# Layer norms of a transformer block: the steps of Pool and ScalarE moved to VectorE, and the low parts of xT taken ahead of the second quarter

## The reference, cut to what matters

```python
def layer_norm(x, g, b):
    xf = x.astype(jnp.float32)
    mu = jnp.mean(xf, -1, keepdims=True)
    xc = xf - mu
    var = jnp.mean(xc * xc, -1, keepdims=True)
    return (xc * lax.rsqrt(var + EPS) * g.astype(jnp.float32) + b.astype(jnp.float32)).astype(x.dtype)

h = layer_norm(ALPHA * h + 0.5 * swiglu(h, ...), ln1_g, ln1_b)   # norm 0
h = layer_norm(ALPHA * h + hybrid_mixer(h, ...), ln2_g, ln2_b)   # norm 1
h = layer_norm(ALPHA * h + 0.5 * swiglu(h, ...), ln3_g, ln3_b)   # norm 2
```

## Time and profile before

| | us |
|---|---|
| median of 3 runs | 2067.95 |
| the single runs | 2066.9, 2067.95, 2069.93 |
| span of the profiled execution | 2066.0 |
| TensorE busy | 2007.9 (97%) |
| VectorE busy | 1103.6 (53%) |
| ScalarE busy | 856.9 (41%) |
| Pool busy | 122.7 (6%) |
| mean granted clock of TensorE | 0.985 of full speed |

### The profile page before, as it was taken

The page is one execution under the profiler, slowest core; times in us unless marked ns, Lnnn a source line. Parts: engine busy times, 40 slices in busy tenths (PEclk is TensorE's granted clock), DMA queues, the critical chain, the costliest instruction groups (busy, mean ns, idle before and its releaser), DMA issues.

```text
span 2066.0 us, 28170 instructions
## 1 busy us (share of the span) xinstructions
PE 2007.9 (97%) x10287; PEld 1711.9 (83%) x10287; DVE 1103.6 (53%) x1232; ACT 856.9 (41%) x957; POOL 122.7 (6%) x134
## 2 busy tenths in 40 slices
PE   8999999999999989999988999899999999999996
PEld 7888888888888879999988977788888888888885
DVE  4555455455544465776384465654555555544455
ACT  4444444444333334445454433344444444433332
POOL 0000000000000032000124210200000000000002
PEclk9999999999999999999999999999999999999998
DMA  7666666665555646655420027366666566555662
GB/s 266 193 186 190 184 182 197 189 191 188 188 173 190 245 124 215 187 163 140 148 82 1 1 83 261 125 197 190 191 187 189 175 194 196 188 172 191 205 210 96
DMA packets 185797, 355.02 MB, mean 172 GB/s; under 512 B 11169, under 2 KB 23553, under 8 KB 184977
## 3 DMA queue, kind: packets, MB, share of 16 engines
q1 hardware_dynamic: 183936, 345.29, 53.6%
q0 software_dynamic: 1696, 8.99, 1.4%
q10 hardware_dynamic: 112, 0.05, 0.0%
HBM read 352.18 MB, written 2.10 MB: 171 GB/s over the span
## 4 chain that ended last, share of the span: by engine, by line
PE 91%; DVE 6%; issue 1%; ACT 1%; POOL 0%; DMA 0%; DVEq 0%; SPq 0%; ACTq 0%; POOLq 0%
PE acc L340 26%; PE acc L342 26%; PE acc L341 26%; PE acc L351 3%; PE acc L355 3%; PE acc L353 3%; PE tp L548 1%; DVE resid L468 1%; PE acc L1726 1%; PE tp L1717 1%; DVE wlo L321 1%; DVE resid L463 1%; DVE resid L648 0%; PE tp L1563 0%; PE tp L378 0%
## 5 line engine op out<-in xcount | busy, mean ns | idle before, releaser
L321 DVE TENSOR_TENSOR wlo<-raw,whi 128x1024 fp32r<-128x1024 f32 (+2 forms) x668 | 798.7, 1203 | 843.5 <-ACT whi L315 843.4
L315 ACT ACTIVATE whi<-raw 128x1024 fp32r<-128x1024 f32 (+2 forms) x668 | 691.1, 1042 | 1025.1 <-PE acc L342 929.0
L340 PE MATMUL acc<-whi,xT 128*128 128x512 f32 (+2 forms) x1728 | 666.5, 386 | 12.8 <-DVE xT L426 9.4
L342 PE MATMUL acc<-whi,xT 128*128 128x512 f32 (+2 forms) x1728 | 660.5, 382 | 0.0
L341 PE MATMUL acc<-wlo,xT 128*128 128x512 f32 (+2 forms) x1728 | 660.2, 382 | 0.0
L340 PEld LDWEIGHTS acc<-whi,xT 128*128 128x128 f32 x1728 | 326.2, 189 | 83.3 <-DVE xT L426 10.3
L342 PEld LDWEIGHTS acc<-whi,xT 128*128 128x128 f32 x1728 | 326.1, 189 | 63.0
L341 PEld LDWEIGHTS acc<-wlo,xT 128*128 128x128 f32 x1728 | 326.3, 189 | 58.6
L340 PE MATMUL acc<-whi,hT 128*128 128x512 f32 x704 | 275.3, 391 | 1.9 <-DVE resid L648 1.9
L342 PE MATMUL acc<-whi,hT 128*128 128x512 f32 x704 | 274.2, 389 | 0.0
L341 PE MATMUL acc<-wlo,hT 128*128 128x512 f32 x704 | 274.0, 389 | 0.0
(11 more groups left out here) (281 smaller groups left out, 1188.9 us busy)
## 6 DMA issues: line engine op xcount, KB each, us to landing
raw<-in_ffn_w_gate_dram SPq DMA_DIRECT2D x176, 512.0 KB, 3.7
raw<-in_ffn_w_up_dram SPq DMA_DIRECT2D x176, 512.0 KB, 3.7
raw<-in_ffn_w_down_dram SPq DMA_DIRECT2D x176, 512.0 KB, 4.2
raw<-in_w_in_dram SPq DMA_DIRECT2D x48, 512.0 KB, 4.0
raw<-in_w_out_dram SPq DMA_DIRECT2D x32, 512.0 KB, 6.2
raw<-in_w_in_dram SPq DMA_DIRECT2D x32, 260.0 KB, 2.9
raw<-in_w_in_dram SPq DMA_DIRECT2D x16, 456.0 KB, 3.6
raw<-in_w_q_idx_dram SPq DMA_DIRECT2D x8, 512.0 KB, 5.5
```

What stands on the lines that cost most here:

```text
L315: act.activation(whi[:, s, :, 0:w], raw[:, r, :, 0:w], ACT.Copy).then_inc(hi_done, 1)
L321: dve.tensor_tensor(wlo[:, s, :, 0:w], raw[:, r, :, 0:w], whi[:, s, :, 0:w].bitcast(F32), ALU.subtract).then_inc(lo_done, 1)
L340: pe.matmul(o, hi, whi[:, s, k, 0:width], start=first and k == 0, stop=False)
L342: ins = pe.matmul(o, lo, whi[:, s, k, 0:width], start=False, stop=last and k == UNIT_KT - 1)
```

## The change

VectorE adds epsilon, ahead of the low part of the weight unit; Pool keeps only the power. `shift` and ScalarE's and Pool's steps on tile 1 of quarters 1 to 3 are gone; VectorE does both tiles in every quarter. At the entries behind norms 0 and 1, VectorE takes the low parts of `xT` from quarter 0 ahead of quarter 1 instead of behind it. The waits of TensorE and of SP's stores count VectorE's steps alone.

```diff
--- before.py
+++ after.py
@@ -246,7 +246,6 @@
         stats = at("stats", cz + 896, [P, T, OUT_CHUNKS, 6])
         mv = at("mv", cz + 1088, [P, T, 2])
         rstd = at("rstd", cz + 1120, [P, T])
-        shift = at("shift", cz + 2496, [P, T])
         half_neg = at("half_neg", cz + 1152, [P, 32])
         ss = at("ss", cz + 1280, [P, 3, T])
         rs = at("rs", cz + 1312, [P, 3, T])
@@ -370,10 +369,8 @@
             if 4 * e + q >= 2:
                 pe.wait_ge(sem("xT_lo"), 4 * e + q - 1)
             for t in range(T):
-                if e > 0 and q == 0:
-                    pe.wait_ge(sem("ln_out"), 5 * (e - 1) + t + 1)
-                elif e > 0:
-                    normed(pe, e - 1, q)
+                if e > 0:
+                    pe.wait_ge(sem("ln_out"), 2 * OUT_CHUNKS * (e - 1) + T * q + t + 1)
                 for k in range(4):
                     ins = pe.transpose(tp[:, 2 * (q % 2) + k // 2, (k % 2) * S + t * P:(k % 2) * S + t * P + P],
                                        resid[:, t, (4 * q + k) * P:(4 * q + k + 1) * P], ident[:])
@@ -414,8 +411,6 @@
 
         def entry_act(act, e, u):
 
-            if u == LEAD - 1:
-                norm_act(act, e - 1)
             q = {LEAD - 1: 0, 2: 1, 4: 2, 6: 3}.get(u)
             if q is not None:
                 to_xT_act(act, e, q)
@@ -439,32 +434,23 @@
             for t in range(T):
                 dve.wait_ge(sem("stats"), T * OUT_CHUNKS * (e + 1))
                 dve.bn_aggr(mv[:, t], stats[:, t]).then_inc(sem("ln_mv"), 1)
+            dve.wait_ge(sem("ln_mv"), 2 * e + 2)
+            dve.tensor_scalar(rstd[:], mv[:, :, 1], EPS / ALPHA ** 2, None, ALU.add).then_inc(sem("ln_rstd"), 1)
             if p is not None:
                 split_lo(dve, p, st.phases[p].iters - 1, st.phases[p].units + LEAD - 1)
             dve.wait_ge(sem("ln_rstd"), 2 * e + 2)
-            dve.scalar_tensor_tensor(out=shift[:], in0=mv[:, :, 0], scalar=-1.0, in1=rstd[:], op0=ALU.mult,
-                                     op1=ALU.mult).then_inc(sem("ln_shift"), 1)
             dve.wait_ge(sem("ln_gains"), 32 * (e + 1))
 
 
-        NORM_STEPS = [2, 3, 4, 5]
-
-        def normed(eng, e, q):
-
-            eng.wait_ge(sem("ln_out"), 5 * e + NORM_STEPS[q])
-            if q >= 1:
-                eng.wait_ge(sem("ln_out_pool"), 3 * e + q)
-
         def norm_quarter(dve, e, q):
 
             cols = slice(q * BANK, q * BANK + BANK)
-            tiles = range(T) if q == 0 else range(1)
-            for t in tiles:
+            for t in range(T):
                 dve.scalar_tensor_tensor(out=resid[:, t, cols], in0=resid[:, t, cols], scalar=mv[:, t, 0:1],
                                          in1=ln_g[:, cols], op0=ALU.subtract, op1=ALU.mult)\
                    .then_inc(sem("ln_mid"), 1)
-            for t in tiles:
-                dve.wait_ge(sem("ln_mid"), 5 * e + NORM_STEPS[q] - len(tiles) + t + 1)
+            for t in range(T):
+                dve.wait_ge(sem("ln_mid"), 2 * OUT_CHUNKS * e + T * q + t + 1)
                 dve.scalar_tensor_tensor(out=resid[:, t, cols], in0=resid[:, t, cols], scalar=rstd[:, t:t + 1],
                                          in1=ln_b[:, cols], op0=ALU.mult, op1=ALU.add)\
                    .then_inc(sem("ln_out"), 1)
@@ -474,8 +460,8 @@
             if u == LEAD - 1:
                 norm_stats(dve, e - 1, (F1D, WO)[e - 1])
                 norm_quarter(dve, e - 1, 0)
+                to_xT_dve(dve, e, 0)
                 norm_quarter(dve, e - 1, 1)
-                to_xT_dve(dve, e, 0)
             elif u == 2:
                 to_xT_dve(dve, e, 1)
                 if e > 0:
@@ -493,29 +479,8 @@
                 pool.dma_start(dst[:], src.to_broadcast([P, D])).then_inc(sem("ln_gains"), 16)
 
         def norm_pool(pool, e):
-            pool.wait_ge(sem("ln_mv"), 2 * e + 2)
-            pool.tensor_scalar(rstd[:], mv[:, :, 1], EPS / ALPHA ** 2, None, ALU.add).then_inc(sem("ln_rstd"), 1)
             pool.wait_ge(sem("ln_rstd"), 2 * e + 1)
             pool.tensor_tensor(rstd[:], rstd[:], half_neg[:, 0:T], ALU.pow).then_inc(sem("ln_rstd"), 1)
-            pool.wait_ge(sem("ln_rstd"), 2 * e + 2)
-            pool.wait_ge(sem("ln_gains"), 32 * (e + 1))
-            for q in range(1, 4):
-                part, step = resid[:, T - 1, q * BANK:q * BANK + BANK], 3 * e + q
-                pool.wait_ge(sem("ln_centred"), step)
-                pool.tensor_tensor(part, part, ln_g[:, q * BANK:q * BANK + BANK], ALU.mult)\
-                    .then_inc(sem("ln_mid_pool"), 1)
-                pool.wait_ge(sem("ln_mid_pool"), step)
-                pool.tensor_tensor(part, part, ln_b[:, q * BANK:q * BANK + BANK], ALU.add)\
-                    .then_inc(sem("ln_out_pool"), 1)
-
-        def norm_act(act, e):
-
-            act.wait_ge(sem("ln_shift"), e + 1)
-            for q in range(1, 4):
-                part = resid[:, T - 1, q * BANK:q * BANK + BANK]
-                act.activation(part, part, ACT.Identity, scale=rstd[:, T - 1:T], bias=shift[:, T - 1:T])\
-                   .then_inc(sem("ln_centred"), 1)
-
 
         GU, DN = [F1GU, F2GU], [F1D, F2D]
 
@@ -1829,10 +1794,7 @@
             for q in range(4):
                 for t in range(T):
 
-                    if t == 0 or q == 0:
-                        sp.wait_ge(sem("ln_out"), 10 + NORM_STEPS[q] - (q == 0) + t)
-                    else:
-                        sp.wait_ge(sem("ln_out_pool"), 6 + q)
+                    sp.wait_ge(sem("ln_out"), 4 * OUT_CHUNKS + T * q + t + 1)
                     cols = slice(q * BANK, q * BANK + BANK)
                     sp.dma_start(out_v[:, t, cols], resid[:, t, cols]).then_inc(sem("stored"), 16)
                     stores += 16
@@ -1865,7 +1827,6 @@
             ffn_act(act, 0, False)
             mixer_act(act)
             ffn_act(act, 1, True)
-            norm_act(act, 2)
 
         @block.vector
         def _(dve):
```

## The result

| | before | after |
|---|---|---|
| median, us | 2068.94 (4 runs) | 2054.73 (4 runs) |
| lowest to highest | 2066.9 to 2070.15 | 2053.11 to 2057.95 |
| span of the profiled execution | 2066.0 | 2051.4 |

The ratio of after to before is 0.9937, with a 95% interval of 0.9925 to 0.9949: 14.2 us faster by the medians, where 14.0 were forecast. A second set of runs of the same kernel gave 0.9934 (0.9920 to 0.9948), with 2053.3 to 2057.6 in five runs.

A forecast was written before the change was run, and what follows sets the result against it. TensorE holds 91% of the path, so layer-norm work counts only where TensorE waits, at norms 0 and 1, and at norm 2. Gains 5.2 + 6.4 + 2.6 - 0.2 = 14.0; 2067.95 - 14.0 = 2054.0, range 2051 to 2059.

The forecast's parts named there:

- Contention as the cause: VectorE's layer-norm steps are long because Pool's resid steps run beside them; about 0.75 each where Pool is done.
- Rival 3: Slower: VectorE's steps are long for a reason of their own and stay at 1.65; 34 slower, 2102; chance 0.03.
- rival 4: Pool's steps were hidden and their removal frees nobody; 2065; chance 0.03, shared with anything not seen.
- Quarter 0 and its way to TensorE: Norms 0 and 1: 4.88 from VectorE's first L463 to TensorE's restart; 4.0 gained at each.
- Epsilon: Epsilon on VectorE, `shift` gone: first step 0.14 earlier at norms 0 and 1, 0.22 saved at norm 2.
- The clock: TensorE's restart at norms 0 and 1: clock likelier to hold at 1.00 than fall, gaining 1.2 and 2.4 more.
- rival 1: The clock falls all the same: at norm 0 alone 2055.2, norm 1 alone 2056.4, both 2057.6; chance 0.32.
- The 1.95 between span and time: Difference between the profiled span, 2066.0, and the median of the runs, 2067.95; kept unchanged in the forecast.
- Late low parts: Quarters 2 and 3: next unit's low part 0.35 late once, mostly taken up next round; 0.2 charged in all.
- VectorE did not become the bound: Rival: VectorE bounds behind the restart, four late quarters each showing 0.5 to 1.35; 2056 to 2059; chance 0.08.
- Norm 2: Last norm, only stores behind it: sixteen shorter VectorE steps, earlier start and one store issue left; 2.6 gained.
- The Trainium skill's rule: Transposes don't count as TensorE being busy, so both clock gains fall away: 10.4 in all instead of 14.0.

## Why the prediction was right

*Contention as the cause* held. The steps fell from 1.65 to 0.74 each where Pool had been beside them, and the two runs with added work of Pool show that it is its reading. Rival 3 (long for a reason of their own) and rival 4 (Pool's steps hidden anyway) are out.

*Quarter 0 and its way to TensorE*: 4.88 forecast from the first L463 to the restart, 4.86 measured at norm 0 (748.98 to 753.84). The sum of durations held to the hundredths, since each link was read from an undisturbed row. The two edits do not add: alone they are worth 1.9 and 2.8 at norm 0, together 4.0. The missing 0.7 is counted twice, because the new shares also shorten quarter 1 from 3.3 to 2.65; on top of them the order is worth 1.2 (8.38 to 7.19) and not 1.9.

*Epsilon*: 0.14 forecast for norms 0 and 1 and 0.22 for norm 2; the first step came 0.13 and 0.20 earlier. Of these the run with epsilon on Pool gives 0.06 and 0.12 to epsilon itself, the rest to `shift`. That the power would be held by the low part was read from L497 and is shown.

*The clock* was the weak step. "Holding is likelier than falling" is not what the runs show: at this restart it held in five places of ten, and both places at once, which I gave more than half, in one profile of five. The size of the term was right where it held (2.5 measured, 2.4 forecast at norm 1). That the sum still came out is luck in part. The forecast had the clock held at both norms, 1.2 of that was missing at norm 0 in the profile, and two other terms made up for it: the end of norm 2, which it had 0.6 too small, and the 1.0 ahead of norm 0, most of it from the clock at the start of the kernel, for which it had nothing. Without these two the span would be 2053.0, and rival 1 with the clock falling at norm 0 alone gives 2066.0 - 12.8 = 2053.2. So the profiled execution shows rival 1 and not the forecast, and the second set of runs of the changed kernel, at 2056.75, lies between rival 1's figures for one fall and for two. The 1.95 between span and time was a little large as well: in the profiled execution after it is 1.7 (2053.11 and 2051.4).

*Late low parts*: charged 0.2, measured 0.35 and 0.16, and the 0.35 at unit 3 is the very figure of the working; it was not taken up in the next round (6.00 against 6.02 before), which is where that estimate erred. VectorE did not become the bound.

*Norm 2*: 2.6 forecast, 3.2 measured. The steps gave 2.18 and 0.20 came first, 2.38 together where 2.29 were worked out; behind the last step 2.85 are left instead of 3.71, where I had counted 0.3 for one issue. The last store now starts alone, 0.7 behind its neighbour, and not side by side with it; that this is the rest of the difference is argued, not shown.

*The Trainium skill's rule* ("TensorE: Matmul & The Clock Gate", Part 4, PE-mode transpose) that transposes don't count as work of TensorE in the same way gave a sum of 10.4. The measured total lies above, but the clock fell often enough that these runs don't decide it: in the changed kernel 3.7 us with nothing but eight transposes stood ahead of the restart, and it held in half of the places.

## What to carry to other kernels

When two engines share a job, compare one instruction's duration with and without the other beside it before counting the split as a gain: here Pool did 18 steps, and 14 of VectorE's 30 took 1.63 to 1.75 instead of 0.74. A helper's tiny step on the path (the power of two numbers) is held just like a large one, so put nothing that reads two SBUF tiles beside it, or let it slip in between short steps. And where TensorE pauses for a few microseconds, look at the granted clock in more than one profile before counting on it: with the restart at 7.2 the gain came at five places of ten, with the restart at 6.3 or sooner at all six.

## What the runs showed that was not expected

Pool's power got its reading in between two back-to-back steps of VectorE: it ended 0.59 behind the first one's end and cost the second nothing, while in the earlier trace rows and in the run with six reading steps Pool's larger steps alternated with VectorE's one to one. The fallen clock lengthens not the matmuls alone but the transposes ahead of them (1.94 for eight instead of 1.23), which moved the restart itself by 0.7. And executions of one kernel differ by up to 5.0 us here (the order alone, 2061.69 to 2066.69). The granted clock is one source of it, also at places that the change did not touch: near 992 us it was down for 10.2 in the profile of the changed kernel and for 13.7 in the second one of the same kernel.
